# One of three buffers for split weights, laid out with high and low words in turn

## The reference

```
proj = hn @ w_in[l]                                  # first block, 9 parts
pre  = jnp.einsum('cd,chkd->chk', hc, u[ec])         # the kernel: all rows of u, then gates
coef = gc * jax.nn.gelu(pre, approximate=False)
out  = jnp.einsum('chk,chkd->cd', coef, v[ec])       # the kernel: all rows of v
a, g = jnp.split(causal_dwconv(h @ w_up, conv_w, conv_b), 2, axis=-1)
(silu(a) * g) @ w_down                               # second block
```

## Time and profile before

| | us |
|---|---|
| median of 3 runs | 1453.69 |
| profiled execution | 1450.47 |
| its span on the core | 1448.7 |
| PE busy | 1401.2 (97%) |
| PEld busy | 1301.1 (90%) |
| DVE busy | 1097.8 (76%) |
| ACT busy | 836.1 (58%) |
| POOL busy | 360.9 (25%) |
| chain that ended last: PE's share | 81% |

### The profile page before, as it was taken

The page is one execution under the profiler, slowest core; times in us unless marked ns, Lnnn a source line. Parts: engine busy times, 40 slices in busy tenths (PEclk is TensorE's granted clock), DMA queues, the critical chain, the costliest instruction groups (busy, mean ns, idle before and its releaser), DMA issues.

```text
span 1448.7 us, 25878 instructions
## 1 busy us (share of the span) xinstructions
PE 1401.2 (97%) x10406; PEld 1301.1 (90%) x10406; DVE 1097.8 (76%) x1903; ACT 836.1 (58%) x1447; POOL 360.9 (25%) x227
## 2 busy tenths in 40 slices
PE   7999999899998999999999999999999999899997
PEld 5998899899998999999988888887889899799997
DVE  7788887567889888999756666677667667797762
ACT  4554774444454677777645445465546666776651
POOL 3216101234445100000032222344322221433200
PEclk9999999899999999999999999999999999999999
DMA  9757775455664544444557666665666536285630
GB/s 386 269 190 268 247 240 176 161 159 179 190 184 146 174 148 147 147 146 146 154 179 221 192 193 196 212 196 181 194 200 245 186 107 199 75 260 176 193 114 30
DMA packets 73721, 268.24 MB, mean 185 GB/s; under 512 B 8401, under 2 KB 9730, under 8 KB 72834
## 3 DMA queue, kind: packets, MB, share of 16 engines
q1 hardware_dynamic: 71280, 256.41, 56.1%
q10 hardware_dynamic: 1426, 7.56, 1.5%
q0 software_dynamic: 896, 2.62, 0.5%
HBM read 262.88 MB, written 3.67 MB: 184 GB/s over the span
## 4 chain that ended last, share of the span: by engine, by line
PE 81%; DVE 12%; ACT 4%; issue 1%; DMA 1%; POOL 1%; DVEq 0%; ACTq 0%; POOLq 0%
PE bank L611 80%; DVE split L1825 3%; DVE ada_acc L1860 2%; ACT split L1295 1%; DVE PR L2275 1%; DMA ringb<-in_w_ada 1%; DVE PR L2272 1%; POOL H L2644 0%; PE bank L784 0%; POOL split L2617 0%; DVE H L2366 0%; DVE PR L2280 0%; DMA vecs<-in_vecs 0%; DVE PA L2076 0%; DVE MH L1927 0%
## 5 line engine op out<-in xcount | busy, mean ns | idle before, releaser
L611 PE MATMUL bank<-H,split 128*128 128x256 f32 x5928 | 732.8, 282 | 15.9 <-DVE split L1825 7.7
L611 PEld LDWEIGHTS bank<-H,split 128*128 128x128 f32 x5928 | 710.2, 189 | 23.5 <-DVE split L1825 9.9
L1295 ACT CAST split<-ringb 128x1024 fp32r<-128x1024 f32 x350 | 365.9, 1047 | 284.5 <-PE bank L611 270.7
L2617 POOL TENSOR_TENSOR split<-ringb,split 128x1024 fp32r<-128x1024 f32 x91 | 229.0, 2517 | 665.7 <-ACT split L1295 665.7
L611 PE MATMUL bank<-split,H 128*128 128x512 f32 (+1 forms) x1728 | 391.1, 388 | 3.3 <-DVE H L2366 1.8
L1825 DVE TENSOR_TENSOR split<-ringb,split 128x1024 fp32r<-128x1024 f32 x259 | 330.9, 1280 | 77.5 <-ACT split L1295 77.4
L611 PEld LDWEIGHTS bank<-split,H 128*128 128x128 f32 x1728 | 321.3, 188 | 71.2 <-POOL split L2617 2.5
L2366 DVE TENSOR_TENSOR H<-PR,H 128x256 fp32r<-128x256 f32 x128 | 137.1, 1074 | 105.5 <-ACT H L1634 105.4
L1825 DVE TENSOR_TENSOR split<-far,split 128x1024 fp32r<-128x1024 f32 x77 | 99.7, 1303 | 33.5 <-ACT split L1295 33.4
L1295 ACT CAST split<-far 128x1024 fp32r<-128x1024 f32 x89 | 92.7, 1047 | 55.1 <-PE bank L611 43.9
L1610 ACT ACTIVATE PR<-bank 128x512 f32<-128x512 f32 (+31 forms) x59 | 28.7, 486 | 76.3 <-PE bank L611 76.3
(11 more groups left out here) (298 smaller groups left out, 1264.0 us busy)
## 6 DMA issues: line engine op xcount, KB each, us to landing
ringb<-in_u SPq DMA_DIRECT2D x128, 512.0 KB, 3.7
ringb<-in_v SPq DMA_DIRECT2D x128, 512.0 KB, 4.4
ringb<-in_w_ada SPq DMA_DIRECT2D x28, 512.0 KB, 5.3
far<-in_w_up SPq DMA_DIRECT2D x26, 512.0 KB, 4.2
far<-in_w_ada SPq DMA_DIRECT2D x20, 512.0 KB, 5.3
ringb<-in_w_up SPq DMA_DIRECT2D x17, 512.0 KB, 4.8
ringb<-in_w_pq SPq DMA_DIRECT2D x16, 512.0 KB, 3.8
far<-in_w_dn SPq DMA_DIRECT2D x14, 512.0 KB, 4.2
```

Source lines behind the costliest of these rows:

```text
L611: return TE.matmul(o, l, r, start=start, stop=stop, skip_group_check=True)
L1295: S.copy(buf(m)[0], slots[P.slot[m]]).then_inc(hi_done, 1)
L2617: G.tensor_tensor(lo, slots[P.slot[m]], hi.bitcast(F32), ALU.subtract).then_inc(lo_g, 1)
```

## The change

The memory of the second buffer's two runs is seen as one run of 2048 words. The high part takes the even words and the low part the odd ones, so that ACT, DVE and POOL write it, and DVE, POOL and PE read it, with a step of two words (8 bytes). The other buffers stay as they were. No instruction is added, removed or moved on any engine, and no DMA touches `split`.

```diff
-        bufs = [(split[:, i, 0, :], split[:, i, 1, :]) for i in range(3)]
+
+        turns = split[:, 1, :, :].rearrange("p z u -> p (z u)").rearrange("p (u z) -> p z u", z=2)
+        bufs = [(split[:, 0, 0, :], split[:, 0, 1, :]), (turns[:, 0, :], turns[:, 1, :]), (split[:, 2, 0, :], split[:, 2, 1, :])]
```

## The result

The changed kernel takes 1574.74 us (median of 4 runs, 1571.78 to 1576.57) against 1453.62 us: slower, ratio 1.084, 95% interval 1.0816 to 1.0864. Its profiled execution took 1571.78 us with a span of 1570.0 us. The predicted time was 1571 us.

A forecast was written before the change was run, and what follows sets the result against it. PE was taken as the bound, by how fast it takes its operands. 552 moving-operand matmuls at half rate add 117.7 us to 1450.5, giving 1568.2, plus 3.2 from profile to median: 1571 us, range 1452 to 1590.

The forecast's parts named there:

- The moving operand: PE's 552 matmuls of 512 columns from the second buffer: 213.3 ns more each, 117.7 us, all on the path.
- the term from above: Upper bound for PE's moving operand: halved rate, 512 x 0.417 = 213 ns more a matmul; the lower bound was 0.
- the fixed part: A matmul's 13.6 ns beyond its columns; hidden behind a slower read it would give back 7.5 us; not counted.
- the speed of sweep: Measure for all five accesses: up to 9.6 bytes a ns costs nothing; PE's moving operand would need 19.2.
- The choice of the upper end: For PE's moving operand, half rate was taken over no cost, since the contiguous read was the nearest row.
- The likeliest case: Moving operand read at about half rate, the rest free: 1571 us, own range 1560 to 1577, chance 0.48.
- the wide range: Whole kernel, over the cases: 1452 to 1590 us, taking in the free case and leaving out the slowed weight load.
- Loads, ACT, DVE and POOL at nothing: Second buffer: PE's weight load, ACT, DVE and POOL accesses at 9.3, 9.5, 7.8 and 3.3 bytes a ns cost nothing.
- its estimate for columns slower by 10%: Weight loads of the second buffer's 79 stationary units: at 10% slower, 121 ns, it would be 6 us.
- The free step: Rival at PE's moving operand in `v`: the step is free everywhere, price 0, time 1453.7; chance 0.33.
- The slowed load: Rival at 1896 weight loads: half rate costs 193 us, 1647 alone or 1765 with the moving term; chance 0.10.
- The slowed DVE: Rival at DVE's subtraction: 1.05 us more each, 8 us in gated `u` plus 12, time 1474; DVE or ACT 0.06.

The follow-up runs named there:

- Runs of four words: Against the kernel before, high and low part take turns in runs of four words in the second buffer's units of `v`: 1454.63 us, ratio 1.0032.
- the step of four: Against the kernel before, the first two buffers share their 4096 words, four parts taking turns word by word in all 250 units: 2126.98 us, ratio 1.4652.
- the two kernels with the streams apart: Kernel before, PE reading 43 units of `v` with even and odd columns from separate places: contiguous 1446.91 us, ratio 0.9974; each with step two 1450.39 us, ratio 1.0001.

## Why the prediction was right

**What bounds the kernel.** Right. PE's steps between matmuls in `v` set the time, and the step in `v` alone, 115.7 us, is most of the 121.1. One reading was wrong: the piece of 240.96 us with 1062 matmuls was taken for the whole stage, which has 128 x 12 = 1536 and lasts 351.5 us. So "near 350 us in place of 241" put the loss of the whole stage on a part of it; the stage went to 467.2 us:

```profile
L613 PE MATMUL bank<-split,H x1536: 387/389/672, 744.7 to 1211.9; 128*128 128x512 f32 x192
```

**The moving operand.** The right term at nearly the right size. 213 ns more a matmul was forecast, 224 measured, so the term from above was a little short; that the fixed part could hide behind the slower read did not happen. 552 x 224 would be 123.6 us. The 36 matmuls of `w_vb`, `w_va` and `w2_mv` are 8.1 us of that and left nothing in the total: the step in `v` alone and in the stationary units alone make 115.7 + 5.9 = 121.6 us, the whole change 121.1. Up to the start of `v` the changed kernel is 4.1 us longer, the one with only the stationary units stepped 4.6. The prediction had said that PE's waits in these stages may hide some of it, and its sum did not count on it.

**The reason given was wrong.** The working took the speed of sweep through the addresses as the limit, 9.6 bytes a ns. Runs of four words sweep twice as fast as a contiguous read and are nearly free; the step of four sweeps twice as fast again and costs a moving operand the same as the step of two; ACT, which the sweep called just within, was slowed by the step of two and not by runs of four. For loads and DVE no run tells the two readings apart. The 9.6 bytes a ns of the contiguous read happened to be the point at which each of two streams has two words of every 16 bytes. The choice of the upper end, called a judgement by little, came out right by this coincidence. The likeliest case had a range of its own, 1560 to 1577, and the measured time is in it, so the wide range was not what saved the forecast; the reason behind the case was luck.

**Loads, ACT, DVE and POOL at nothing.** Wrong by some 5.9 us for the loads. A load went from 188 to between 196 and 200 ns, and with 118.0 ns a matmul there was hardly room. The prediction named this as a sign of being wrong, a load longer than 191 ns in a third of the units, and it came true; its estimate for columns slower by 10%, 6 us, is what was found, but it was left out of the sum. ACT's cast, forecast to stay at 1.05 us, went to between 1.12 and 1.14 in the second buffer; in `v` its wait for PE covers it:

```profile
L1297 ACT CAST split<-ringb x125: 1047/1048/1137, 744.6 to 1198.7; 128x1024 fp32r<-128x1024 f32 x125
```

DVE's subtraction stayed at 1.22 us. The misses add up: 516 x 10.7 ns = 5.5 us too little on the long matmuls of `v` and 5.9 for the loads, against 36 x 213.3 ns = 7.7 us counted for the three small stages, leave the 3.7 us between 1571 and 1574.7. So the close agreement is in part errors that cancel.

**The rivals.** The free step, 0.33, fell: the Trainium skill's rule (SBUF — State Buffer, Specifications (TRN2)) of two hits in 16 bytes fits the load, which loses 4 to 6% with a step of two words and takes 1.4 ns a column with three and 1.9 with four, but it does not hold for the moving operand as a whole: there two hits took 451 ns for 227. Nor is a step of four words free for any access that these runs timed, where the Trainium skill's note on cachelines (SBUF — State Buffer, Door 1: The DMA port swizzle) has it free for float32. The slowed load, 0.10, is there at 3% of the price that was set on it. The slowed DVE, 0.06, fell; the Trainium skill's rule on pairs of adjacent words (Vector Engine (DVE) Microarchitecture Reference, 5.2 Measured stream behaviour on trn2) does not hold for a step of two, 1.22 us as before. With a step of four DVE took 2.04 us; three was not run.

## What to carry to other kernels

Where matmuls bound a kernel, look at how the moving operand lies in SBUF: in these float32r matmuls everything that left the even and the odd columns with one word in each 16 bytes halved the rate (451 to 460 ns for 227). In a stationary operand a step of two words cost 8 to 12 ns a load, but a step of three 74 and of four 141. Cost a moving operand per stream and per 16 bytes, and not by the bytes it spans. When a contiguous float32 matmul takes some ns more than its columns at the clock, try an order that gives even and odd columns each a contiguous run.

## What the runs showed of the hardware that was not expected

- The moving operand behaves as two streams, even and odd columns, each with 16 bytes about every 1.8 ns: 451 ns for 512 columns at a step of two words and 460 at four (1.76 and 1.80 ns a column of one stream), 227 for two streams of step two in separate places, 451 to 458 for runs of four words begun 8 bytes off.
- A contiguous float32 read seems itself held by this: 226.9/512 x 4 = 1.77 ns for 16 bytes. For it speak the two kernels with the streams apart: with two words used of each 16 bytes the step is 227 ns again, with four it is 215.
- ACT's writes behave as a single stream of this kind; weight loads and DVE fit it too, but no run parts it from a limit on sweep for them. At a step of four words: load 0.86 to 1.9 ns a column, ACT's cast 1.05 to 2.04 us, DVE's subtraction 1.22 to 2.04, POOL's only 2.40 to 2.92.
- Beside a moving operand with the step, loads of a contiguous operand last 208 in place of 188 ns. Whether the two reads of PE share something or the load waits for the slower matmul was not tested.
